# Sums of squares of q and k from a high and a low part, their eviction on ScalarE, and two groups of transposes moved by a quarter

## The reference, cut to what matters

```python
aq, ak, av, mq, mk, mv, mi, mf, mo = split_in(xn @ w_in)
aq = rms_norm(aq.reshape(B, T, H_ATT, 2, DQK_ATT), q_norm_g)   # y * rsqrt(mean(y*y) + 1e-6) * g
ak = rms_norm(ak.reshape(B, T, H_ATT, 2, DQK_ATT), k_norm_g)   # over the 128 elements of each half head
k_all = jnp.concatenate([cache_k[l].astype(k_new.dtype), k_new], axis=1)   # 256 cached keys per stream
s = jnp.einsum('bqhcd,bkhcd->bchqk', q, k) * (DQK_ATT ** -0.5)
```

## Time and profile before

| | before |
|---|---|
| median of 3 runs | 1822.22 us (1817.82 to 1823.04) |
| the profiled execution | 1822.9 us |
| its span, first to last instruction | 1821.1 us |
| TensorE matmuls | 1804.1 us busy (99%), 9716 instructions |
| TensorE weight loads | 1626.5 us (89%) |
| VectorE | 877.3 us (48%) |
| ScalarE | 682.0 us (37%) |
| GpSimd | 137.2 us (8%) |
| mean granted TensorE clock | 0.995 of full speed |
| DMA traffic | 251 MB, mean 138 GB/s |

### The profile page before, as it was taken

One profiled execution on the slowest core, in us unless ns is written; L12 is line 12 of the kernel. 1 busy time (PEld: TensorE's weight loads), 2 busy tenths in 40 slices (PEclk: granted clock), 3 DMA queues, 4 the chain that ended last, 5 costly groups with the idle time before them and its releaser, 6 DMA issues.

```text
span 1821.1 us, 28082 instructions
## 1 busy us (share of the span) xinstructions
PE 1804.1 (99%) x9716; PEld 1626.5 (89%) x9716; DVE 877.3 (48%) x1678; ACT 682.0 (37%) x1296; POOL 137.2 (8%) x182
## 2 busy tenths in 40 slices
PE   8999999999999999999999999999999999999998
PEld 6999999999987778999888999888999888999887
DVE  4533675455556555555433444433455433555333
ACT  5223554444445435433333333333333333333332
POOL 3110000000111000011000011000011000111000
PEclk8999999999999999999999999999999999999999
DMA  7574346665666443344344444344444344444442
GB/s 173 148 197 125 96 106 204 200 184 150 189 171 195 150 126 118 112 125 125 127 127 127 126 119 124 127 127 127 124 119 125 127 127 127 123 120 126 145 144 93
DMA packets 297366, 251.42 MB, mean 138 GB/s; under 512 B 9312, under 2 KB 244128, under 8 KB 297264
## 3 DMA queue, kind: packets, MB, share of 16 engines
q1 hardware_dynamic: 281736, 210.07, 40.1%
q0 software_dynamic: 11088, 37.25, 6.3%
q10 hardware_dynamic: 4472, 3.16, 0.7%
HBM read 234.87 MB, written 15.56 MB: 138 GB/s over the span
## 4 chain that ended last, share of the span: by engine, by line
PE 97%; ACT 1%; DVE 1%; DMA 0%; issue 0%; POOL 0%; ACTq 0%; DVEq 0%; POOLq 0%
PE acc L496 17%; PE acc L498 17%; PE acc L497 17%; PE bank L581 8%; PE bank L582 8%; PE bank L580 8%; PE bank L1715 4%; PE bank L1722 2%; PE ssb L580 2%; PE ssb L581 2%; PE ssb L582 2%; PE ssb L1715 1%; PE bank L542 1%; PE bank L541 1%; PE bank L543 1%; PE acc L541 1%
## 5 line engine op out<-in xcount | busy, mean ns | idle before, releaser
L478 DVE TENSOR_TENSOR w_lo<-raw,w_hi 128x512 fp32r<-128x512 f32 x768 | 559.2, 735 | 856.5 <-ACT w_hi L469 855.9
L469 ACT ACTIVATE w_hi<-raw 128x512 fp32r<-128x512 f32 x768 | 483.8, 631 | 892.2 <-PE acc L498 450.8
L496 PE MATMUL acc<-x2g_hi,w_hi 128*128 128x384 f32 x1024 | 347.2, 339 | 1.0 <-DVE x2g_lo L1628 1.0
L498 PE MATMUL acc<-x2g_hi,w_lo 128*128 128x384 f32 x1024 | 346.5, 338 | 0.0
L497 PE MATMUL acc<-x2g_lo,w_hi 128*128 128x384 f32 x1024 | 346.0, 338 | 0.0
L496 PE MATMUL acc<-a_hi,w_hi 128*128 128x400 f32 (+1 forms) x768 | 272.8, 355 | 0.0
L497 PE MATMUL acc<-a_lo,w_hi 128*128 128x400 f32 (+1 forms) x768 | 264.5, 344 | 0.0
L498 PE MATMUL acc<-a_hi,w_lo 128*128 128x400 f32 (+1 forms) x768 | 264.1, 344 | 0.0
L580 PE MATMUL bank<-w_hi,a_hi 128*128 128x512 f32 x640 | 252.3, 394 | 1.5 <-DVE w_lo L478 1.5
L581 PE MATMUL bank<-w_lo,a_hi 128*128 128x512 f32 x640 | 253.1, 395 | 0.0
L582 PE MATMUL bank<-w_hi,a_lo 128*128 128x512 f32 x640 | 252.7, 395 | 0.0
(11 more groups left out here) (327 smaller groups left out, 1538.6 us busy)
## 6 DMA issues: line engine op xcount, KB each, us to landing
raw<-in_w_up SPq DMA_DIRECT2D x128, 512.0 KB, 4.1
raw<-in_w_down SPq DMA_DIRECT2D x128, 512.0 KB, 3.9
raw<-in_w_in SPq DMA_DIRECT2D x96, 512.0 KB, 4.1
raw<-in_w_out SPq DMA_DIRECT2D x32, 512.0 KB, 3.9
kc<-in_cache_k POOLq DMA_DIRECT2D x8, 1024.0 KB, 6.5
vc<-in_cache_v POOLq DMA_DIRECT2D x8, 1024.0 KB, 9.0
C_rows<-in_state_C POOLq DMA_DIRECT2D x8, 512.0 KB, 7.0
out<-C_rows POOLq DMA_DIRECT2D x8, 512.0 KB, 5.0
```

Source lines behind the costliest of these rows:

```text
L469: e.activation(w_hi[:, q], raw[:, slot, 4 * (q % 2):4 * (q % 2) + 4, :], ACT.Copy).then_inc(hi_ready, 1)
L478: e.tensor_tensor(w_lo[:, q], raw[:, slot, 4 * (q % 2):4 * (q % 2) + 4, :], w_hi[:, q].bitcast(F32), ALU.subtract).then_inc(lo_ready, 1)
L496: e.matmul(out, w_hi[:, q, kk], hi[:, k, at], start=k == 0, stop=False, skip_group_check=True)
L498: last = e.matmul(out, w_lo[:, q, kk], hi[:, k, at], start=False, stop=k == KT - 1, skip_group_check=True)
```

## The change

1. The squares of pair u are split: ScalarE squares into `n_sq` and copies that to `n_hi` (fp32r), VectorE subtracts to get `n_lo` (fp32r). TensorE multiplies both with an fp32r matrix of ones, two one-pass matmuls per half in place of one fp32 matmul.
2. The square and its high part for pair u+1 are made by ScalarE in q=3 of the tile before (for u=0, ahead of tile 16). VectorE makes `n_lo` in q=0 of the pair's own tile. TensorE's sums stay in q=1 and wait for `n_low`.
3. ScalarE evicts the sums, with scale and eps, at the head of its q=2 work; VectorE's eviction in q=1 is gone.
4. The second part of a stream's cached keys is transposed one slot ahead of its scores in place of two, and "ko" of block j at slot 4j+3 in place of 4j+2.
5. Small: GpSimd copies ones to `ones_r` once at the start; VectorE sets a column to eps.

```diff
-KEYS_AT = (-4, -2)
+KEYS_AT = (-4, -1)
...
-    plan += [(4 * (j - AV_AHEAD), "av", j) for j in range(AV_AHEAD, 8)] + [(4 * j + 2, "ko", j) for j in range(8)]
+    plan += [(4 * (j - AV_AHEAD), "av", j) for j in range(AV_AHEAD, 8)] + [(4 * j + 3, "ko", j) for j in range(8)]
...
         # gpsimd
+            e.tensor_copy(ones_r[:], ones[:]).then_inc(S("ones_r_made"), 1)
...
         # scalar
-            e.wait_ge(S("st_set"), 1)
+            e.wait_ge(S("st_set"), 2)
...
+            def n_square(u):
+
+                cols = pair_cols(u)
+                e.activation(n_sq[:, :, cols], zt[:, 2 * u:2 * u + 2, cols], ACT.Square).then_inc(S("n_sq_made"), 1)
+                e.wait_ge(S("n_sq_made"), u + 1)
+                e.activation(n_hi[:, :, cols], n_sq[:, :, cols], ACT.Copy).then_inc(S("n_squared"), 1)
+
             def qk_norm(t, q):
 
                 u = t - T_AV
                 cols = pair_cols(u)
-                if q == 0:
-                    if u:
-                        done(e, ("n", u - 1, 1))
-                    e.activation(n_sq[:, :, cols], zt[:, 2 * u:2 * u + 2, cols], ACT.Square).then_inc(S("n_squared"), 1)
+                if q == 3 and u + 1 < 8:
+                    done(e, ("n", u, 1))
+                    e.wait_ge(S("n_low"), u + 1)
+                    n_square(u + 1)
                 elif q == 2:
+                    for x in range(2):
+                        b = take(e, ("n", u, x))
+                        taken(e.activation(n_mean[:, x, cols], b[:, cols], ACT.Identity, scale=1.0 / DQ,
+                                           bias=eps_col[:, 0:1]), ("n", u, x))
                     read_out(e, ("n", u, 0), ("n", u, 1))
                     e.activation(n_root[:, :, cols], n_mean[:, :, cols], ACT.Ln).then_inc(S("n_logged"), 1)
...
+            n_square(0)
             for t in range(T_AV, T_M):
                 split_hi(e, (t + 1) // 2, (t + 1) % 2, after=lambda q: qk_norm(t, q))
...
         # vector
+            e.memset(eps_col[:], EPS).then_inc(S("st_set"), 1)
...
-                if q == 0 and u >= 2:
-                    take_av(u - 2)
-                elif q == 1:
-                    for x in range(2):
-                        b = take(e, ("n", u, x))
-                        ins = ts(n_mean[:, x, cols], b[:, cols], 1.0 / DQ, EPS, ALU.mult, ALU.add)
-                        taken(ins, ("n", u, x))
+                if q == 0:
+                    e.wait_ge(S("n_squared"), u + 1)
+                    if u:
+                        done(e, ("n", u - 1, 1))
+                    tt(n_lo[:, :, cols], n_sq[:, :, cols], n_hi[:, :, cols].bitcast(F32),
+                       ALU.subtract).then_inc(S("n_low"), 1)
+                    if u >= 2:
+                        take_av(u - 2)
                 elif q == 3:
...
         # tensor
                 elif q == 1:
-                    e.wait_ge(S("n_squared"), u + 1)
+                    if u == 0:
+                        e.wait_ge(S("ones_r_made"), 1)
+                    e.wait_ge(S("n_low"), u + 1)
                     for x in range(2):
                         b = fill(e, ("n", u, x))
-                        filled(mm(b[:, pair_cols(u)], ones[:], n_sq[:, x, pair_cols(u)], True, True), ("n", u, x))
+                        mm(b[:, pair_cols(u)], ones_r[:], n_hi[:, x, pair_cols(u)], True, False)
+                        filled(mm(b[:, pair_cols(u)], ones_r[:], n_lo[:, x, pair_cols(u)], False, True), ("n", u, x))
```

More of the change, by code:

```diff
@@ L316, in build @@
         ones = sb("ones", [P, P])
+        ones_r = sb("ones_r", [P, P], F32R)
         rstd_x = sb("rstd_x", [P, TOK])
         o_rows = sb("o_rows", [P, 2, DV])
+        eps_col = sb("eps_col", [P, 1])
         ocol = sb("ocol", [P, 2, 6])
@@ L357, in build @@
             vc = sb("vc", [P, 2, 2, NH * DV], scope=s)
+            with ExitStack() as s_n:
+                n_hi = sb("n_hi", [P, 2, TOK], F32R, scope=s_n)
+                n_lo = sb("n_lo", [P, 2, TOK], F32R, scope=s_n)
             kT = sb("kT", [P, 8, PAST], scope=s)
```

## The result

| | before | after |
|---|---|---|
| median | 1822.63 us (1817.82 to 1824.92, 4 runs) | 1870.47 us (1865.0 to 1875.44, 4 runs) |
| ratio | | 1.0269 [1.0236, 1.0302] |
| span of the profiled execution | 1821.1 us | 1866.7 us |
| TensorE busy, share of the span | 99% | 97% |
| mean granted TensorE clock | 0.995 | 0.989 |

The change costs 48 us, 2.7%. The forecast was 1861, in a range of 1840 to 1878; the measured time is also 0.5 us above its inner range, 1852 to 1870.

The account below looks back on a forecast made before the run. TensorE, busy throughout tiles 16 to 41, was taken as the bound; +21 (low part, with the sums' saving), +11.5 (moved transposes) and +7 (clock) gave 39.5 us, forecast 1861 us, range 1840 to 1878, inner range 1852 to 1870.

Parts of the forecast that it names:

- What bounds the kernel: Tiles 16 to 41: TensorE is always busy, so work removed from it or waits given to it count in full.
- Part 1, the sums: Norm tiles: four one-pass matmuls replace two fp32 sums, saving 0.63 us a tile, 5.0 us in eight.
- Part 2, the low part: Norm sums: n_lo behind VectorE's Newton chain makes TensorE wait 3.7 us; +21 us in all, saving included.
- step of 0.94 us for ScalarE's evictions: ScalarE's quarter 2: evicting both sums first makes Ln, and all behind it, 0.94 us later.
- Part 3, the moved transposes: Attention slots: merging groups gains nothing, and shared banks 4 and 1 make TensorE wait; +11.5 us.
- the fall of the clock in attention: Attention's waits: taken as the shorter sort, without a clock fall, priced at 0.
- the hand-off of the keys to the scores: Attention: the keys' last evictions, a quarter later, stay hidden ahead of the scores, with 1.2 us to spare.
- Part 4, the clock: Seven waits of 3.7 us at the norm's sums: four clock falls of 1.7 us each taken, +7 us.
- The bound of 12 for seven falls: Norm sums: upper bound of the clock's cost, seven falls at 1.7 us each, 12 us.
- the clock falls at every wait: Rival: seven falls at the sums and a few more at slots 11 to 27, giving 1872; chance 0.12.
- The sum: Whole kernel: terms 21, 11.5 and 7 add to 39.5 us on the profiled execution's 1822.9; forecast 1861.
- the low part is ready in time: Rival, norm sums: n_lo ends before 243.75 and banks go in time, leaving only 5.0 us saved: 1817; chance 0.06.

Follow-up runs that it names:

- early_parts: Against norm_only: ScalarE's square and high part of the next pair moved to quarter 1, VectorE's low part to quarter 2, a tile ahead; 1816.75 us, ratio 0.9968.
- low_first: Against norm_only: VectorE makes the next pair's low part in quarter 3 ahead of the Newton chain, ScalarE's eviction waits for n_done; 1825.38 us, ratio 1.0006.
- kept_busy: Against norm_only: 18 matmuls with unused results ahead of TensorE's wait for the low part, in seven tiles; 1845.56 us, ratio 1.0131.
- vector_evicts: Against norm_only: VectorE evicts the sums in quarter 1 as before, ScalarE's two evictions gone; 1844.76 us, ratio 1.0096.
- turns_only: Against the kernel before: only the second part of the keys and ko moved to their later slots; 1837.29 us, ratio 1.0080.
- norm_only: Against the changed kernel: keys and ko back in their slots of before, leaving the norm's part alone; 1858.82 us, ratio 1.0207.

## Why the prediction held, and where it was off

**What bounds the kernel:** right. Every wait that TensorE was given was paid in full, and later stages gave nothing back: from the last score product with cached keys to the end are 1368.3 us before and 1368.1 after.

**Part 1, the sums:** right. 0.18 us a matmul, 0.58 to 0.63 us saved a tile (early_parts), the lower value at 384 columns.

**Part 2, the low part:** right in place and mechanism, and low_first is the proof: with the same work ahead of the Newton chain 30 of the 33 us are gone. The waits were forecast at 3.7 us and are 3.5 to 4.0 by the records. The term of +21 measures +23 (kept_busy against the kernel before: 23.7 in the stretch of the norms, 0.5 of it the wait for kT). Its step of 0.94 us for ScalarE's evictions was 1.16 by the trace, which is 1.5 us in seven tiles. vector_evicts took 0.9 to 1.3 us off each wait.

**Part 3, the moved transposes:** right in mechanism, banks 4 and 1, slot by slot. The term of +11.5 measures 12.0 (the stretch of attention, 191.2 against 179.2). Two things in it were priced too low: the fall of the clock in attention, which turns_only had once and the changed kernel didn't, and the hand-off of the keys to the scores, "1.2 us to spare". In the changed kernel TensorE waited 1.06 us there once, at slot 4, for VectorE's copy of the keys (the row for `kT` among the waits): VectorE had the mask's 2.3 us and the tile's eviction ahead of it. The step looked at ScalarE and the longest chain of transposes, not at what VectorE has in that quarter.

**Part 4, the clock:** right that it falls, too low in count and in price. "I take four falls, +7 us": there were six in seven waits, one of them twice as long. The windows miss 11.9 us of full speed, and the time that this cost is 9.3 us (norm_only less kept_busy in the stretch of the norms). The bound of 12 for seven falls left out that one can last longer than the 3.4 us that was seen. The forecast rested on one wait of 1.5 us without a fall and one of 2.7 with; the twelve traces have that same wait of 2.7 with and without one, so two waits of one trace could not settle it. The trace of before also had the fall at 517.6, without a wait, which the prediction didn't look at.

The Trainium skill (TensorE: Matmul & The Clock Gate, The HAM clock gate) says that the throttled state is the default and activity releases it. Six of the seven waits of 3.5 to 4.0 us agree with that and one doesn't; in the count of falls it was the better guide.

The rival "the clock falls at every wait" said 1872 and is nearer to the 1870 measured than the forecast's 1861, but by luck: it priced the clock at 17 us, 12 at the sums and 5 in attention, where none fell in the changed kernel. At 9.3 measured, the forecast's 7 is the nearer price.

**The sum** of the stretches is 33.6 us for the norms (23.7 the low part with 0.5 of the wait for kT, 9.3 the clock, 0.6 the rest of the wait for kT) and 12.0 for attention; the profiled spans differ by 45.6, the medians by 47.8, and the forecast had 39.5. Of the 6 us between the forecast and the spans the clock is 2.3, the low part 2, the hand-off of the keys 1.1 and the turns 0.5. The 2 us more of the medians are not explained by a trace; they are about the size of one fall.

**The rivals on the other side:** "the low part is ready in time" needed `n_lo` before 243.75 in the old trace's time. The change's order doesn't give that; early_parts does, and lands at 1816.75, where this rival had put it (1817). That it is so close is luck in part: the edit itself is worth 4.1 us.

## What to carry to other kernels

An engine that is half idle can still be late at one place. Before its instruction is put on the path of the bound engine, read what stands ahead of it in that quarter, not its busy share. Where data are known early, make them early: the same instructions a tile ahead turned +33 us into -4 in their stretch (+35 into -7 by the medians). Two groups that share a bank need the eviction's time between them, and DMA issues on the evicting engine's queue count as part of that time. Where the change puts waits of 2 us and more between dense matmuls, price a fall of the clock with each: here seven such waits cost 9 us by the clock alone. Before a difference of some us is put down to an edit, look at the stretches that the edit doesn't touch.

## What was not expected of the hardware

TensorE's clock fell to 1.2 GHz in six of seven tiles with waits of 3.5 to 4.0 us, and also in six with waits of 2.2 to 2.8 us, between dense matmuls; it did not with waits of 0.3 to 1.0 us (low_first, kept_busy). In attention it fell once, behind the pair of 0.74 and 1.03 us at slot 11 of turns_only, and did not behind the same pair in the changed kernel. Four of the changed kernel's six falls began while TensorE was idle, two 1.5 us after it had started again. Most falls lasted 3.4 us; the one at the first long wait lasted 6.8 in all three kernels that had such waits unfilled. Eighteen matmuls whose results nobody reads, put into each of seven waits, made the stretch of the norms 9.3 us shorter (norm_only to kept_busy). An eviction from PSUM by ScalarE with scale and bias took 0.58 us at 400 columns, a plain copy of 384 columns 0.47.
